# A decode tile on raw weights: four fp32 column groups in place of twelve F32R products

## What is computed

```python
# layer 0, retention mixer; h is x*(1+scale)+shift, T = 512 prompt tokens or 1 sample token
q, k, v, g = split(h @ w_in_ret)               # 1024 x 6144, fp32
o, s = retention_scan(rot(q), rot(k), v, s0)   # for a sample: s = gamma*s0 + k^T v, o = q s
y = (group_norm(o) * silu(g)) @ w_out_ret      # 2048 x 1024
# layer 1, DSA mixer
q, k, v, qi, ki, wi = split(h @ w_in_dsa)      # 1024 x 2640
o = sparse_attend(...)
y = o @ w_out_dsa                              # 1024 x 1024
# after every mixer and every expert layer
x = layer_norm(ALPHA * x + gate * y)           # shift, scale, gate from silu(c) @ w_mod + b_mod
```

## Time and profile before

| | |
|---|---|
| median of 3 runs | 2047.05 us (2037.37 to 2049.27) |
| profiled execution, its own time | 2051.82 us |
| its span | 2050.1 us |
| mean granted TensorE clock | 0.889 |
| busy: PE, DVE, ACT | 1720.3, 1244.4, 871.4 us |

### The profile page before, as it was taken

One profiled execution on the slowest core, in us unless ns is written; L12 is line 12 of the kernel. 1 busy time (PEld: TensorE's weight loads), 2 busy tenths in 40 slices (PEclk: granted clock), 3 DMA queues, 4 the chain that ended last, 5 costly groups with the idle time before them and its releaser, 6 DMA issues.

```text
span 2050.1 us, 22707 instructions
## 1 busy us (share of the span) xinstructions
PE 1720.3 (84%) x7697; PEld 1195.8 (58%) x7697; DVE 1244.4 (61%) x1824; ACT 871.4 (43%) x1028; POOL 101.0 (5%) x149
## 2 busy tenths in 40 slices
PE   3779999999999984999997579997887929999970
PEld 0546546774577632878774366554626728877760
DVE  1432364433654356988884823588524868988867
ACT  1222233333341043888773422333622227888841
POOL 0000010000000002000001100001000020000001
PEclk8789999999999976999998569997957959999995
DMA  9456763216523469999998411115001539999953
GB/s 334 176 198 229 265 248 114 93 62 210 200 100 118 133 240 347 369 392 393 391 392 307 157 65 62 42 36 171 1 21 41 176 127 388 392 392 393 391 204 125
DMA packets 200177, 435.29 MB, mean 212 GB/s; under 512 B 15961, under 2 KB 20073, under 8 KB 199054
## 3 DMA queue, kind: packets, MB, share of 16 engines
q1 hardware_dynamic: 174338, 339.04, 46.2%
q0 software_dynamic: 18384, 73.10, 9.4%
q10 hardware_dynamic: 7374, 22.12, 3.2%
HBM read 379.96 MB, written 66.85 MB: 218 GB/s over the span
## 4 chain that ended last, share of the span: by engine, by line
PE 58%; DMA 16%; DVE 11%; ACT 5%; issue 5%; DVEq 3%; ACTq 1%; POOL 0%; SPq 0%; POOLq 0%
PE bank L688 27%; PE bank L1080 12%; DMA RING<-in_w_gate 5%; DMA RING<-in_w_up 4%; PE bank L672 4%; DMA RING<-in_w_mod 3%; ACT WH L1606 2%; DVE WL L2427 2%; DMA RING<-in_w_in_ret 2%; PE bank L710 2%; PE bank L981 1%; PE bank L1005 1%; DMA RING<-in_w_in_dsa 1%; PE bank L679 1%; PE bank L1206 1%
## 5 line engine op out<-in xcount | busy, mean ns | idle before, releaser
L2427 DVE TENSOR_TENSOR WL<-RING,WH 128x2048 fp32r<-128x2048 f32 x192 | 435.8, 2288 | 64.3 <-ACT WH L1606 63.2
L688 PE MATMUL bank<-RINGR,HTH 128*128 128x512 f32 (+3 forms) x1440 | 465.1, 406 | 0.9 <-DVE HTL L1990 0.5
L1606 ACT ACTIVATE WH<-RING 128x2048 fp32r<-128x2048 f32 x192 | 364.9, 1915 | 119.7 <-PE bank L1080 96.5
L688 PEld LDWEIGHTS bank<-RINGR,HTH 128*128 128x128 f32 (+1 forms) x1440 | 247.8, 180 | 106.8 <-issue 27.7
L688 PE MATMUL bank<-RINGR,HTL 128*128 128x512 f32 (+3 forms) x720 | 287.7, 400 | 0.0
L672 PE MATMUL bank<-cst,M 128*128 128x128 f32 (+3 forms) x721 | 116.9, 294 | 152.9 <-DMA M<-h_d 54.6
L1981 DVE TENSOR_TENSOR RINGR<-RING,RINGR 128x2048 fp32r<-128x2048 f32 (+1 forms) x48 | 105.6, 2213 | 181.7 <-ACT RINGR L1375 181.5
L1080 PE MATMUL bank<-WH,HGH 128*128 128x512 f32 x512 | 204.5, 399 | 4.7 <-DVE HGL L2436 4.7
L672 PEld LDWEIGHTS bank<-cst,M 128*128 128x128 f32 (+3 forms) x721 | 94.2, 158 | 188.2 <-DMA M<-h_d 55.6
L1080 PE MATMUL bank<-WH,HGL 128*128 128x512 f32 x512 | 201.3, 393 | 0.0
L1080 PE MATMUL bank<-WL,HGH 128*128 128x512 f32 x512 | 201.2, 393 | 0.0
(11 more groups left out here) (306 smaller groups left out, 2220.4 us busy)
## 6 DMA issues: line engine op xcount, KB each, us to landing
RING<-in_w_gate SPq DMA_DIRECT2D x64, 1024.0 KB, 11.6
RING<-in_w_up SPq DMA_DIRECT2D x64, 1024.0 KB, 12.3
RING<-in_w_down SPq DMA_DIRECT2D x64, 1024.0 KB, 11.4
RING<-in_w_mod SPq DMA_DIRECT2D x48, 1024.0 KB, 9.0
RING<-in_w_in_ret SPq DMA_DIRECT2D x24, 1024.0 KB, 5.6
RING<-in_state_ret SPq DMA_DIRECT2D x16, 1024.0 KB, 6.6
out_ret_sample<-RING POOLq DMA_DIRECT2D x16, 1024.0 KB, 6.0
h_d<-y_d POOLq DMA_DIRECT2D x8, 1536.0 KB, 7.1
```

What stands on the lines that cost most here:

```text
L688: last = pe.matmul(out, x_[:, c, :], w_[:, c, :], start=start and c == n == 0, stop=stop and c == 3 and n == 2)
L1606: act.activation(WH[:, u % SPLIT, :, :], raw(u % RAW), ACT.Copy).then_inc(S("hi_rdy"), 1)
L2427: TT(WL[:, u % SPLIT, :, :], raw(u % RAW), WH[:, u % SPLIT, :, :].bitcast(F32), ALU.subtract)\
```

## The change

The tile with 8 tokens leaves the split path in 34 of the 48 units: in the retention blocks k to v1 and g1 of both hp and q of hp = 1 (18 units), the 8 units of `out0`, the units of `D_ORDER[1]` and `[2]` (4), and the 4 units of `out2`. In their place `few_unit` multiplies the *raw* unit in fp32 with `DX` (or `DXY` for y), one chunk in each of four column groups, and sums over the units of a block in one bank. ACT copies that bank (`take_few`), and one fp32 product with `C("sel")` (`few_sum`) adds the four groups in the place of tile 4 of the last unit. As `low` overwrites the raw unit, `few_unit` of a unit stands one unit ahead, after t = 0 of the unit before, and `low` waits for it (`few_ps`). To free bank 3 the transposes use bank 2 alone, and the conditioning part has one buffer `MP` in place of two. In `mixer_close` the `low`s of n = 1 are moved, and in the DSA projections `low` of two h = 1 units goes behind the rotations. In the state loop the value row is kept as high and low half in 40 partitions (`VHL`), and the spread is one F32R product with `pick` for each half of the columns.

```diff
+        FEW_BLOCKS = [blk for blk in range(len(BLOCKS)) if blk and blk % 6 != 4]
+        FEW = [BLOCKS[blk] + (h,) for blk in FEW_BLOCKS for h in range(2)] + [("out0", n, kq) for n in range(2) for kq in range(4)] \
+            + [("din", D_ORDER[i], h) for i in (1, 2) for h in range(2)] + [("out2", n, kq) for n in range(2) for kq in range(2)]
...
+            def few_unit(key):
+
+                wait_slot(pe, key)
+                bk, x_, first, final = bank[3], DX, key[-1] == 0, FEW_AT[key] in FEW_LAST
...
+                if first:
+
+                    pe.wait_ge(S("few_ev"), sum(i < FEW_AT[key] for i in FEW_LAST))
+                w = slot(key)
+                for c in range(4):
+                    last = pe.matmul(bk[32 * c:32 * c + DEC, :], x_[:, 4 * key[-1] + c, :], w[:, c, :], start=first, stop=final)
+                last.then_inc(S("few_ps"), 1)
+
+            def few_sum(out, part):
+
+                nonlocal taken
+                taken += 1
+                pe.wait_ge(S("few_ev"), taken)
+                return pe.matmul(out[0:DEC, :], C("sel")[:, 0:DEC], part[:, :], start=True, stop=True)
...
             def ret_unit(blk, key, h, before, after):
...
-                    last = unit_mm(bank[D_BANK[t]][0:rows(t), :], *h_tile(t, h), key + (h,), h == 0, h == 1)
+                    if t < NT or not few:
+                        last = unit_mm(bank[D_BANK[t]][0:rows(t), :], *h_tile(t, h), key + (h,), h == 0, h == 1)
+                    elif h:
+                        last = few_sum(bank[D_BANK[t]], FEW_RET)
                     if h == 1:
                         last.then_inc(S("ret_mm"), 1)
-                    elif t == NT:
+                    elif t == (NT - 1 if few else NT):
                         last.then_inc(S("ret_half"), 1)
+                    if t == 0:
+                        following = key + (1,) if h == 0 else unit_after(blk)
+                        if following in FEW_AT:
+                            few_unit(following)
...
-                if yt >= 2:
-
-                    pe.wait_ge(S("yt_ev"), yt - 1)
-                transposes([bank[2 + yt % 2][:, q * R:(q + 1) * R] for q in range(4)],
+                if yt:
+
+                    pe.wait_ge(S("yt_ev"), yt)
+                transposes([bank[2][:, q * R:(q + 1) * R] for q in range(4)],
...
                     if b == 0:
-                        pe.wait_ge(S("qk_rd"), hp + 1)
+                        pe.wait_ge(S("q_step"), 2 * hp + 2)
+                        pe.wait_ge(S("v_step"), 3 * hp + 3)
...
-                        pe.matmul(bank[1 + hh][:, :], ident[0:DEC, b:b + 1].to_broadcast([DEC, P]),
-                                  V[0:DEC, NT, hh * NB:(hh + 1) * NB], start=True, stop=True).then_inc(S("vb_ps"), 1)
+                        pe.matmul(bank[1 + hh][:, :], pick[:, b:b + 1].to_broadcast([32 + DEC, P]),
+                                  VHL[:, hh * NB:(hh + 1) * NB], start=True, stop=True).then_inc(S("vb_ps"), 1)
...
+                act.wait_ge(S("v_step"), 3 * hp + 1)
+                act.wait_ge(S("ret_ev"), (6 * hp + 4) * TILES)
+                act.activation(VHL[0:DEC, :], V[0:DEC, NT, :], ACT.Copy).then_inc(S("v_step"), 1)
...
             def low(*key):
 
                 dve.wait_ge(S("w_hi"), place[key][5] + 1)
+                if key in FEW_AT:
+
+                    dve.wait_ge(S("few_ps"), FEW_AT[key] + 1)
...
             def mixer_close(m):
                 T = EPT[m]
-                if m == 2:
-                    low("out2", 1, 0)
-                    low("out2", 1, 1)
+                low(f"out{m}", 1, 0)
                 dve.wait_ge(S("ep_in"), 64 * m + 64)
...
-                if m == 0:
-                    low("out0", 1, 0)
-                    low("out0", 1, 1)
                 for t in range(TILES):
                     add_half(0, t)
+                low(f"out{m}", 1, 1)
+                if m == 2:
+
+                    dve.wait_ge(S("kv_st"), 16 * 3 * TILES)
+                fold(m, HN[1])
                 if m == 0:
                     low("out0", 1, 2)
                     low("out0", 1, 3)
-                else:
-
-                    dve.wait_ge(S("kv_st"), 16 * 3 * TILES)
-                fold(m, HN[1])
...
+                few = i + 1 < 6 and ("din", D_ORDER[i + 1], 1) in FEW_AT
+                if i + 1 < 6 and not few:
                     low("din", D_ORDER[i + 1], 1)
                 for t in range(TILES):
                     rotate_d(i, t)
                     index_step(i, 1, t)
+                if few:
+                    low("din", D_ORDER[i + 1], 1)
```

More of the change, by code:

```diff
@@ L457, in trunk @@
         CT = over("CT", [P, KD, 32], F32, QM_AT, D)
-        MP = [over(f"MP{i}", [P, NB], F32, QM_AT, i * NB) for i in range(2)]
+        MP = over("MP", [P, NB], F32, QM_AT, 0)
+        DX = sb("DX", [P, KD, DEC])
+        DXY = view(24 * TOK + NT * NB + TILES * 2 * NB + 3 * NB, 2 * KD, DEC)
+        FEW_RET = over("FEW_RET", [P, NB], F32, QM_AT, NB)
+        FEW_OUT = {0: RO, 2: PT[0].rearrange("p a b -> p (a b)")}
+        VHL = over("VHL", [32 + DEC, 2 * NB], F32R, QM_AT, 0)
+        pick = sb("pick", [32 + DEC, DEC], F32R)
         stage = over("stage", [DEC + 1, 4, NB], F32, SC_AT, 0)
@@ L722, in late_sum @@
                 if pending:
-                    mod_sum(mod_at - 1, MP[(mod_at - 1) % 2], bank[7])
+                    mod_sum(mod_at - 1, MP, bank[7])
                 pending = False
@@ L739, in next_mods @@
                 for k in steps:
-                    banks = (bank[4], bank[5]) if g == 0 else (bank[1], bank[3])
+                    banks = (bank[3], bank[5]) if g == 0 else (bank[1], bank[3])
                     if k == 0:
@@ L799, in d_unit @@
                 w = unit_width(key)
-                last = unit_mm(bank[D_BANK[t]][0:rows(t), 0:w], *h_tile(t, h), key, h == 0, h == 1)
+                few = key in FEW_AT
+                if t < NT or not few:
+                    last = unit_mm(bank[D_BANK[t]][0:rows(t), 0:w], *h_tile(t, h), key, h == 0, h == 1)
+                elif h:
+                    last = few_sum(bank[D_BANK[t]], FEW_OUT[2])
                 if h == 1:
                     last.then_inc(S("d_mm"), 1)
-                elif t == NT:
+                elif t == (NT - 1 if few else NT):
                     last.then_inc(S("d_half"), 1)
+                if t == 0 and i:
+                    following = ("din", D_ORDER[i], 1) if h == 0 else ("din", D_ORDER[i + 1], 0) if i < 5 else None
+                    if following in FEW_AT:
+                        few_unit(following)
             def router(m, t):
@@ L819, in out_product @@
                         for t in range(TILES):
-                            if kq == 0 and n == 1 and t >= 3:
-                                pe.wait_ge(S("out_ev"), TILES * m + t - 2)
-                            last = unit_mm(bank[O_BANK[n][t]][0:rows(t), :], xh[:, :, cols(t)], xl[:, :, cols(t)],
-                                           (f"out{m}", n, kq), kq == 0, kq == quarters - 1)
+                            if n == 1 and (kq == 0 and t in (2, 3) or kq == quarters - 1 and t == NT):
+                                pe.wait_ge(S("out_ev"), TILES * m + t - 1)
+                            if t < NT:
+                                last = unit_mm(bank[O_BANK[n][t]][0:rows(t), :], xh[:, :, cols(t)], xl[:, :, cols(t)],
+                                               (f"out{m}", n, kq), kq == 0, kq == quarters - 1)
+                            elif kq == quarters - 1:
+                                last = few_sum(bank[O_BANK[n][t]], FEW_OUT[m])
                             if n == kq == 0:
@@ L828, in out_product @@
                                 last.then_inc(S("out_mm"), 1)
-                            elif t == NT:
+                            elif t == NT - 1:
                                 last.then_inc(S("out_half"), 1)
+                            if t == 0:
+                                following = (f"out{m}", n, kq + 1) if kq < quarters - 1 else (f"out{m}", 1, 0)
+                                if (n, kq) != (1, quarters - 1):
+                                    few_unit(following)
             pe.nop().then_inc(S("unit_used"), UNIT0)
@@ L905, in turn_qk @@
                     pe.wait_ge(S("ro_rdy"), qk + 1)
-                    if qk >= 2:
-                        pe.wait_ge(S("qk_ev"), qk - 1)
+                    if qk:
+                        pe.wait_ge(S("qk_ev"), qk)
                     isk = (qk // TILES) % 2
                     src = KN[:, t, :] if isk and t < NT else RO
-                    transposes([bank[2 + qk % 2][:, q * R:(q + 1) * R] for q in range(4)],
+                    transposes([bank[2][:, q * R:(q + 1) * R] for q in range(4)],
                                [src[0:R, q * P:(q + 1) * P] for q in range(4)], "qk_ps")
@@ L1362, in turned @@
                     act.wait_ge(S("ht_ps"), 2 * TILES * m + 2 * t + g + 1)
+                    if m % 2 == 0 and t == NT:
```

(7 more changed lines are left out.)

69 lines of the change are left out of this document (55 added, 14 removed).

## The result

The changed kernel takes 2064.1 us (median of 4 runs, 2063.4 to 2065.7), the kernel before 2046.1 (4 runs, 2037.4 to 2049.3): ratio 1.0099, interval 1.0082 to 1.0116. It is 1% slower; 2025 had been predicted, at most 2050. The profiled execution has a span of 2062.1 us against 2050.1.

What follows compares the result with a forecast made beforehand. PE was taken to bound the kernel, except where blocks q to v1 of hp = 0 wait for loads. Terms 21 - 20 - 13.9 - 0.2 - 10 + 0.8 + 0.3 = -22 us gave 2029.8 profiled, 2025 median; range 1994 to 2050.

Steps and rivals of the forecast that it cites:

- the step "that costs": Blocks q to v1 of hp = 0: PE waits in few_unit for the next unit's load; +21 us (0 to +32).
- hp = 1: -13.9: Blocks g1 of hp = 0, q to v1 and g1 of hp = 1: 12 units cheaper, 6 sums added; -13.9 us.
- The books: PE's times as if nobody waited: 34 units of 2.78 us removed, few_unit and few_sum added; net 41 us less.
- DSA: -10: DSA projections: DVE's low goes behind the rotations, so PE's idle and slow clock shrink; -10 us (-4 to -12).
- Value rows: -20: State loop: two F32R products replace two fp32 ones, step falls from 7.81 to 6.5 us; -20 us (-8 to -21).
- Output product: -0.2: Output product: gain of 11.3 us given back by +11.1, as low of (1, 2) stands behind fold; -0.2 us.
- if I am wrong on the order: Output product: alternative in which low of (1, 2) behind fold costs nothing; -11.3 us.
- `few_unit` of 1.1 us: Each of 34 few_unit on PE, four fp32 products in four column groups, takes 1.1 us; nearest bounds 0.97 and 1.94.
- (a): Rival: loads of hp = 0 are there when few_unit asks, fold isn't late; 1993, or 2004 for hp = 0 alone; chance 0.25.
- (c): Rival: few_unit's four column groups run one after another, 3.8 us each; +92 us, 2117; chance 0.05 with the unforeseen.
- (b): Rival: units 1 to 6 of hp = 0, POOL's pieces shift into load bursts; 26 us more, 2051; chance 0.15.

Runs made afterwards that it cites:

- e2: Changed kernel with the column groups left out of blocks k, v0 and v1 of hp = 0 alone: 2030.1 us.
- e4: Changed kernel with the next unit's column groups behind t = 2, not t = 0, in blocks q to v1 of hp = 0: profiled span 2018.5 us.
- e9: e7 with split and low of the second halves of k and v0 of hp = 1 ahead of the previous block's fifth tile: blocks between state loops 174.1 us.
- e7: Changed kernel with the edits of e3 and e4, and the output product's first few_unit ahead of t = 0 of the last retention unit: ratio 0.9758.
- e3: Changed kernel with DVE's low of (out0, 1, 2) and (1, 3) ahead of fold, and ACT's DSA column-group copy ahead of the split: median fell by 26.6 us.
- e1_values: Kernel before with the value rows' part alone (F32R product of 40 rows), no column groups: ratio 0.9926.
- e5_no_retention: Changed kernel with the two orders of e3 and the column groups left out of all retention blocks: 2015.1 us.

## Why the prediction was wrong

The steps that failed are three terms of the sum: blocks q to v1 of hp = 0, the blocks of hp = 1, and the DSA projections. Together they turned -22 into +12. For the first the mechanism was right and its size too small. In the other two, waits that the prediction hadn't named took the gain: for hp = 1 the overlap was wrong (what ran on DVE under the fifth tile's 2.78 us), for DSA the queue of ACT was left out.

- **hp = 0, the step "that costs": +21, measured +35.6** (+31 to +38 by the spread of the stage), beyond the end of 32 that it was given. One part is arithmetic: from 181.67 to 232.99 it is 51.3 us and not 49.8, so the terms as they stand give +19, and 16.5 us are missing. Four things were short. The landings: 10.3, 8.4, 10.4, 9.4, 10.3 and 9.5 us after the start of units 1 to 6, 58.2 in sum for 53.4. I had read even units by the moment at which the DMA engines fall silent; in the changed kernel PE goes on 0.8 to 1.9 us after that. The clock: `few_unit` behind a wait runs at half of it, and the slow stretches with the next tile cost 14.8 us in all, for 12.3. And "odd units of q and k waited before too ... and now wait for the same load at another place": no, they wait at both. The rotation still stands behind `low`, and on DVE `low` stands behind the conditioning sum, which PE now reaches later: 2.1 us each in units 1 and 3, with 1.6 us of slow clock behind the second. Last, PE's sum and partial products of the conditioning, taken as "2" for the unit, brought waits of 0.3 to 0.8 us for their bank and for `low`, 2.5 in all. The four make 4.8 + 2.5 + 5.8 + 2.5 = 15.6 us. e2 and e4 show that it is this place and nothing else.
- **hp = 1: -13.9, measured +1.2.** "Loads run two units ahead there, so `few_unit` finds its unit": true, and not enough. The books are right: 10 units of 2.78 gone, 8 `few_unit` of 1.17 and 5 sums of 1.05 in the 138 us behind g1's first tile, -13.2, plus 5.95 of waits and slow clock is -7.2, measured -7.0. The stretch before it, from g0 on, lost 4.2: two `few_unit`, 0.4 us of idle and 1.6 of slow clock. g0 and g1 of hp = 1 lost 3.9, with three `few_unit`, one of them the output product's, and 3.2 us of idle. What I didn't ask was who else lived in the fifth tile's 2.78 us. The prediction had asked it for the transposes' bank, and for `fold`; not for `low` behind a rotation and not for `y_low` behind `few_unit`. e9 gives 4 to 5.6 us back, e7 4.3. With both the two stages take 234.4 us for the 243.1 before, -8.7; some 2 of the 5.2 us that are still missing are the thirteenth `few_unit` and 1.17 us in place of 1.1, and 1.8 the two new waits of 0.9 us.
- **DSA: -10, measured -3.8** (87.0 to 83.2). The idle at i = 0 shrank as forecast (9.9 to 7.6 us); at i = 1 I had moved DVE's `low`, and didn't follow ACT's queue, in which the copy that frees the bank for the next column groups stands behind a split. 7.5 us, given back by e3; with it the stretch is 11.3 us shorter than before.
- **Value rows: -20, measured -18.7.** The step is 6.56 us for 6.5, the spread 0.66 for 0.6. No other engine is late but in the first step of each loop, where PE waits 0.64 us for `qk_t`; 0.5 had been set aside for that.
- **Output product: -0.2, measured -1.4**, of which 1.2 is the `few_unit` that stands in g1; idle 8.6 us for 8.9. e3 gives the whole 11.6 back, as the alternative "if I am wrong on the order" had it.
- **`few_unit` of 1.1 us**: 0.97 and some 0.2 for the changes of form around it. The estimate from the Trainium skill's figures (TensorE: Matmul & The Clock Gate, "Measured speedup vs the span model") had made it 1.2 us, and the traces don't bear that out: each `few_unit` that doesn't follow a wait takes 0.97 or 0.98 us to the next start, so the row of the state loop stands for this place too.
- **The rivals.** (a) falls: the loads were late. (c) falls: 0.97 us. (b), the slower side, gave its reason wrongly: in the changed kernel unit 1 has no piece of POOL beside its load and lands after 10.3 us, units 3 and 5 have one, issued 0.9 us before the unit, and land after 10.4 and 10.3. The second piece comes 9.6 and 9.7 us after the load has landed, so nothing collides. Where a second piece does fall into the burst, as in the kernel before (issued at 143.62 and 191.22 us), units 3 and 5 land 11.9 and 13.3 us after their start, against 9.6 for unit 1. That (b)'s size, 26 us more in this stage, was nearer than the forecast's is luck. That so little chance was left above 2050, half of (b) and the 0.05 of (c), was the real fault: three terms each rested on the claim that one queue was all there was to look at, and they could only err to the slow side.

## What to carry to other kernels

Work that is brought forward to a place between two tiles brings its waits with it: ask when its operand is there, and put it behind that moment (here, behind t = 2 in place of t = 0: 38 to 42 us). Work that is taken off the bounding engine was also the time in which the other queues caught up: go through each queue for the instructions that had finished only just in time, by the margin between their end and the start that needed them, before the saving is booked. And an instruction that only frees a buffer must not stand in a queue behind one that waits for a load.

## What the runs showed that was not expected

The length of an idle doesn't tell alone whether the clock falls behind it. The 85 idles of 5 to 9.3 us in these twelve traces were all followed by 0.50. But idles of 1.7 and 2.0 us in the changed kernel were followed by 0.64, the first with twelve products in 4.5 us, while one of 2.5 us was followed by 1.00:

```profile
350.30:355.00 4.70, 4.70 (x18) 3.74 (x17) 4.33 (x8) 1.09 (x2) 0.00 (x0) 0.64 0.37 154
429.30:434.00 4.70, 4.70 (x16) 3.44 (x20) 0.00 (x0) 0.08 (x1) 0.00 (x0) 0.64 0.53 202
461.40:465.00 3.60, 3.56 (x20) 2.29 (x20) 0.00 (x0) 0.47 (x1) 0.00 (x0) 1.00 0.49 189
```

What ran before the idle doesn't tell either. e3_order has the same instructions up to there and the same idles of 1.69 and 2.50 us, and its clock behind them is the other way round:

```profile
424.90:429.60 4.70, 4.70 (x24) 2.90 (x25) 0.62 (x1) 0.93 (x3) 0.00 (x0) 1.00 0.51 194
455.40:460.10 4.70, 4.67 (x16) 3.38 (x20) 0.00 (x0) 0.12 (x1) 0.00 (x0) 0.66 0.37 141
```

And the idle of 2.05 us at the place of the first row had 1.00 behind it in the kernel before and in e1_values, but 0.64 in e5_no_retention, where no column groups run in these blocks:

```profile
312.90:317.60 4.70, 4.70 (x18) 3.68 (x17) 4.33 (x8) 1.08 (x2) 0.00 (x0) 0.64 0.38 158
```

So behind such short idles the 1.7 us of slow clock come in one execution and not in another, and a single trace can't credit them to an edit.
